# Spatial gate of a two-layer hybrid block: the bias as a tile added on VectorE, and the four mixing banks each behind another dense block

## The chip, the cores and the metric

The kernel runs on one NeuronCore of one Trainium2 chip. The metric is the device time of one launch in microseconds (us). The engines are TensorE (PE in the trace, its weight loads PEld), VectorE (DVE), ScalarE (ACT), GpSimd (POOL) and the DMA queues, issued by SyncE (SP). TensorE's granted clock is 1.00 (2.4 GHz) or 0.50 (1.2 GHz); a number between is a mean over a stretch.

## What is computed

Two layers on 1024 tokens of width 1024. The first projects the normalised input onto 7168 columns, runs four branches on parts of them (a short convolution, a stick-breaking attention, an RWKV-7 scan and a spatial gate), merges them under sigmoid gates, and ends with a gated feed-forward net with a convolution. The second is an attention layer. The change touches the spatial gate, branch four:

```python
def spatial_gating(z, ln_g, ln_b, w_s, b_s):
    u, v = jnp.split(jax.nn.gelu(z), 2, axis=-1)          # (1, 1024, 256) each
    v = layer_norm(v, ln_g, ln_b)
    vb = v.reshape(bsz, t // 128, 128, 4, 64)
    w_causal = jnp.tril(w_s)                               # (4, 128, 128)
    mixed = jnp.einsum('gts,bnsgc->bntgc', w_causal, vb) + b_s.T[:, :, None]
    return u * mixed.reshape(bsz, t, 256)
```

So in each of 8 groups of 128 positions, each of 4 channel groups of 64 is mixed over the positions by its own lower triangular 128x128 matrix; a bias that depends on the position in the group and the channel group is added; and the result is multiplied by u.

## The kernel before

**Dense blocks.** All large products are made of blocks. A block (`whole`, which calls `product`, lines 927 to 929) takes 1024x128 weights from a ring of two slots, each split into a high and a low part (`w_hi`, `w_lo`), and 8 x 2 x 3 = 48 products of 128x128 by 128x512: high by high, low by high, high by low, summed in PSUM. Its result [128 columns, 1024 tokens] lies in one of the two halves of the PSUM tile `gp` (block t in half t mod 2) and raises `p_ready`. ScalarE or VectorE takes it from there and raises `p_free0` or `p_free1`, for which block t+2 waits. GpSimd splits the weights of block t+1 once block t-1 is done; SyncE loads them from HBM (`w_raw`).

**The input projection** is 16 blocks (`for t in range(T_GATE)`), in the order of `IN_ORDER`: t = 0, 1 are u of the spatial gate (`y_d`), t = 2, 3 its v (`vt_sg`), t = 4, 5 the attention's v (`vt_sb`), t = 6 to 11 the short convolution (t = 10 and 11 are taken by VectorE, the others by ScalarE), t = 12 to 15 the attention's q and k. Then 32 gate blocks follow, of another loop, with pieces of the attention between their halves.

**Small work between the blocks.** The other half of PSUM is `sm`, four banks of [128, 512]. TensorE is given small work there between dense blocks, by hand: after t = 0 `col_turns` (parameters turned to columns), after t = 1 `bias_turns` (lines 1009 to 1015, the attention bias of the second layer, three products), after t = 4 and t = 7 `turn_v` (16 transposes each, v of the spatial gate and of the attention), and after t = 9 `sg_mix` (lines 1028 to 1043). Once VectorE has turned v to tokens x channels (line 2039), it normalises it in place in `v_sg` and raises `sg_normed` (line 2059).

`sg_mix` fills bank after bank, bank b = (ft, half) with channels 128 ft to 128 ft + 127 of tokens 512 half to 512 half + 511. A bank is four groups, one for each 128 tokens:

```python
pe.matmul(sm[:, b, c], group_sel[:, ft, :], sg_bias[:, :], start=True, stop=False, ...)       # line 1037
for hh in range(2):
    mm = pe.matmul(sm[C*hh:C*hh+C, b, c], v_sg[:, tt, C*g:C*g+C], w_sg[:, g, :], start=False, ...)  # line 1041
```

The first product puts the bias there: `group_sel` [4, 2, 128] selects for each channel its group's row of `sg_bias` [4, 128]. The other two are the mixing of two channel groups, which go to the two halves of the partitions. After a bank, `sg_mixed` goes up, and VectorE multiplies the bank by u into `y_d` (line 2071) and raises `sg_done`. Nothing before the first gate block waits for `sg_done`; there TensorE waits for four.

**VectorE's order** there is: `bias_vec` (line 2022) which SyncE stores and TensorE waits for ahead of `turn_v`; copies of v, its norm; v of the attention (line 2065, `v_taken`); the four gate products (line 2071); then for t = 10 and t = 11 the short convolution (lines 2078 to 2085), each of which first takes the block out of PSUM (line 2078) and so frees it.

Of the kernel before, what the change touches and what calls it, by code (L numbers as in the profile page):

```python
# [7 lines left out]
P = 128  # L8
# [6 lines left out]
BT = BW // P  # L15
C = 64
# [18 lines left out]
ALU = mybir.AluOpType  # L35
ACT = mybir.ActivationFunctionType
F32 = mybir.dt.float32
# [150 lines left out]
def hybrid_layers(nc, x, mix_norm_g, w_in, gate_b, sc_conv_w, sc_out, sb_out, rw_mu, rw_w0, rw_w2,  # L188
# [9 lines left out]
    with ExitStack() as ctx:  # L198
        base = [-(-nc.sbuf_base // 32) * 32]

        def at(name, shape, dtype, offset):
            return nc.alloc_sbuf_tensor_at(name, shape, dtype, offset=offset)
# [15 lines left out]
        group_sel = fixed("group_sel", [4, 2, P])  # L218
# [11 lines left out]
        sg_bias = fixed("sg_bias", [4, P])  # L230
# [42 lines left out]
        v_sg = at("v_sg", [P, NB, BW], F32, A0 + 40 * K)  # L273
        w_sg = at("w_sg", [P, 4, P], F32, A0 + 64 * K)
        gate_out = at("gate_out", [P, 2, T], F32, A0 + 56 * K)

# [636 lines left out]
        def _(pe):  # L913
# [94 lines left out]
            def bias_turns():  # L1008
                pe.wait_ge(s["rel_in"], 32)
                wait("wsg_copied")  # L1010
                wait("cols")
                for n in range(3):
                    mm = pe.matmul(sm[0:HEADS_A, n, 0:384], rel_rows[0:33, :],
                                   buckets[0:33, 384 * n:384 * n + 384], start=True, stop=True)
                mm.then_inc(s["bias_p"], 1)
# [11 lines left out]

            def sg_mix():
                wait("sg_normed")
                wait("wsg_ready")  # L1030
                pe.wait_ge(s["v_taken"], 8)
                for b in range(4):
                    ft, half = divmod(b, 2)
                    for n in range(4):
                        tt = 4 * half + n
                        c = slice(P * n, P * n + P)
                        pe.matmul(sm[:, b, c], group_sel[:, ft, :], sg_bias[:, :], start=True, stop=False,
                                  skip_group_check=True)
                        for hh in range(2):
                            g = 2 * ft + hh  # L1040
                            mm = pe.matmul(sm[C * hh:C * hh + C, b, c], v_sg[:, tt, C * g:C * g + C], w_sg[:, g, :],
                                           start=False, stop=True, skip_group_check=True)
                    mm.then_inc(s["sg_mixed"], 1)

            for t in range(T_GATE):
# [8 lines left out]
                if t == 7:  # L1054
                    pe.wait_ge(s["v_taken"], 4)
                    turn_v(vt_sb, 3)
                if t == 9:
                    sg_mix()

# [931 lines left out]
        def _(dve):  # L1991
# [19 lines left out]
            for i in range(16):  # L2011
# [8 lines left out]
            dve.tensor_copy(w_sg[:, :, :], sm[:, 1, :].rearrange("p (g t) -> p g t", g=4)).then_inc(s["wsg_copied"], 1)  # L2020
            wait("bias_p")
            dve.tensor_scalar(bias_vec[:, :].rearrange("p (n c) -> p n c", n=3), sm[0:HEADS_A, 0:3, 0:384],
                              -1.0, None, ALU.mult).then_inc(s["bias_rows"], 1)
# [38 lines left out]
            for b in range(4):  # L2062
# [3 lines left out]
                                sm[:, b, :].rearrange("p (n c) -> p n c", n=4)).then_inc(s["v_taken"], 1)  # L2066
            for b in range(4):
                ft, half = divmod(b, 2)
                c = slice(HALF * half, HALF * half + HALF)
                wait("sg_mixed")  # L2070
                dve.tensor_tensor(y_d[:, ft, c], sm[:, b, :], y_d[:, ft, c], ALU.mult).then_inc(s["sg_done"], 1)
            for n in range(2):
                t = IN_ORDER.index(4 + n)
# [7 lines left out]
                for shift in (1, 2):  # L2081
                    wait.after(dve.scalar_tensor_tensor(
                        acc[:, shift:T], cx[:, 0:T - shift], pcol("sc_w", 4 - 2 * shift + n),
                        acc[:, shift:T], ALU.mult, ALU.add))
                ins = dve.tensor_tensor(y_a[:, n, :], y_a[:, n, :], acc, ALU.mult)
            ins.then_inc(s["sc_done"], 1)

# [540 lines left out]
```

## Time and profile before

| | us |
|---|---|
| runs shown | 2606.4, 2625.24, 2626.96 |
| median of them | 2625.24 |
| the profiled execution, its own time | 2625.7 |
| span of its trace | 2623.8 |
| TensorE busy | 2508.9 (96%) |
| VectorE, ScalarE, GpSimd busy | 1051.2, 607.9, 823.9 |
| mean granted clock of TensorE | 0.971 |

The span is the time from the first to the last instruction in the trace; 1.9 us of the execution lie around it. Starts are counted from the span's start. Of TensorE's work the dense products of lines 927 to 929 are the most: 1600 of each line into `gp` and 352 into `sm`. A product of plain float32 operands stands in the trace as two instructions, so that one product of line 1037 reads "x2" and the two of line 1041 read "x4". The time that a product costs its successor is the distance of their starts; the duration in a row is longer, since products overlap.

### The profile page before, as it was taken

How to read it: one execution, taken by the hardware profiler on the slowest of the kernel's cores; microseconds unless marked ns; L12 is line 12 of the kernel's file. 1: busy time of each engine (PE TensorE's matmuls, PEld its weight loads, DVE VectorE, ACT ScalarE, POOL GpSimd, SP SyncE). 2: the span in 40 equal slices, each digit the busy share in tenths (PEclk: the TensorE clock that was granted, in tenths of full speed). 3: DMA queues.
4: the chain of work that ended last, by engine and by line, in shares of the span. 5: the costliest groups of instructions: out<-in, count | busy, mean ns of one | idle time of the engine just before them, and what ended most of it. 6: DMA issues, size and time to landing. Idle time of an engine off the chain costs nothing.

```text
span 2623.8 us, 36062 instructions
## 1 busy us (share of the span) xinstructions
PE 2508.9 (96%) x15586; PEld 1985.3 (76%) x15586; DVE 1051.2 (40%) x1275; ACT 607.9 (23%) x901; POOL 823.9 (31%) x518
## 2 busy tenths in 40 slices
PE   7999999999999979999999999999899989979998
PEld 6878777777778767888888888887677866646676
DVE  4211122241385264344444444444443216675521
ACT  3101122322222111121111111112322015554410
POOL 4312333233232057633333333332632310131221
PEclk9989999999999689999999999999999999989999
DMA  5111322222100055311111111111113122000023
GB/s 193 41 33 48 97 81 81 76 70 80 57 18 4 2 184 184 89 41 48 49 49 49 49 50 49 48 48 40 48 41 104 40 64 46 1 8 1 1 61 116
DMA packets 194122, 156.89 MB, mean 60 GB/s; under 512 B 15674, under 2 KB 175649, under 8 KB 193738
## 3 DMA queue, kind: packets, MB, share of 16 engines
q1 hardware_dynamic: 193994, 155.00, 19.5%
q8 instruction: 103, 1.69, 0.3%
q14 instruction: 25, 0.20, 0.0%
HBM read 125.58 MB, written 29.40 MB: 59 GB/s over the span
## 4 chain that ended last, share of the span: by engine, by line
PE 85%; DVE 8%; POOL 3%; ACT 2%; issue 1%; DMA 0%; SPq 0%; POOLq 0%; DVEq 0%; ACTq 0%
PE gp L927 18%; PE gp L929 17%; PE gp L928 17%; PE sm L929 4%; PE sm L927 4%; PE sm L928 4%; PE sm L1581 2%; PE gp L1484 2%; PE gp L1500 2%; POOL merged L824 2%; PE sm L1517 2%; DVE att_s L2466 1%; PE sm L1089 1%; PE sm L1439 1%; PE sm L1068 1%
## 5 line engine op out<-in xcount | busy, mean ns | idle before, releaser
L927 PE MATMUL gp<-h_hi,w_hi 128*128 128x512 f32 x1600 | 639.0, 399 | 1.3 <-ACT k_sb L1669 1.3
L929 PE MATMUL gp<-h_hi,w_lo 128*128 128x512 f32 x1600 | 624.3, 390 | 0.0
L928 PE MATMUL gp<-h_lo,w_hi 128*128 128x512 f32 x1600 | 624.0, 390 | 0.0
L726 POOL CAST w_hi<-w_raw 128x1024 fp32r<-128x1024 f32 (+1 forms) x165 | 176.1, 1067 | 1147.0 <-PE gp L929 821.0
L728 POOL TENSOR_TENSOR w_lo<-w_raw,w_hi 128x1024 fp32r<-128x1024 f32 x173 | 432.6, 2500 | 124.1 <-ACT w_hi L1822 101.9
L927 PEld LDWEIGHTS gp<-h_hi,w_hi 128*128 128x128 f32 x1600 | 301.0, 188 | 84.1 <-issue 23.6
L928 PEld LDWEIGHTS gp<-h_lo,w_hi 128*128 128x128 f32 x1600 | 301.1, 188 | 64.8 <-issue 4.5
L929 PEld LDWEIGHTS gp<-h_hi,w_lo 128*128 128x128 f32 x1600 | 300.9, 188 | 64.1
L2092 DVE TENSOR_TENSOR_SCAN sb_run<-sb_keep,ones_row 128x128 f32<-128x128 f32 (+7 forms) x32 | 77.1, 2449 | 318.2 <-POOL sb_keep L773 318.2
L927 PE MATMUL sm<-h_hi,w_hi 128*128 128x512 f32 x352 | 136.9, 389 | 0.0
L928 PE MATMUL sm<-h_lo,w_hi 128*128 128x512 f32 x352 | 136.9, 389 | 0.0
L929 PE MATMUL sm<-h_hi,w_lo 128*128 128x512 f32 x352 | 136.9, 389 | 0.0
L1929 ACT ACTIVATE att_s<-att_s,small 128x1024 f32<-128x1024 f32 (+7 forms) x128 | 98.7, 773 | 28.3 <-DVE small L2466 27.5
L1843 ACT ACTIVATE hid<-gp,col 128x1024 f32<-128x1024 f32 x22 | 24.6, 1119 | 325.9 <-DVE gp L2339 325.9
L1581 PE MATMUL sm<-k_tile,q_tile 96*128 96x512 f32 (+3 forms) x192 | 71.4, 509 | 20.0 <-DVE small L2466 13.9
L1484 PE MATMUL gp<-ident,att_s 128*128 128x128 f32 x576 | 79.0, 280 | 7.7 <-DVE att_pt L2486 7.7
L2339 DVE TENSOR_TENSOR gp<-gp,sin_t 128x1024 f32<-128x1024 f32 x22 | 27.1, 1233 | 131.0 <-PE gp L929 119.3
L1484 PEld LDWEIGHTS gp<-ident,att_s 128*128 128x128 f32 x576 | 61.7, 141 | 21.4 <-issue 10.3
L928 PEld LDWEIGHTS sm<-h_lo,w_hi 128*128 128x128 f32 x352 | 66.1, 188 | 13.7
L929 PEld LDWEIGHTS sm<-h_hi,w_lo 128*128 128x128 f32 x352 | 66.1, 188 | 13.7
L927 PEld LDWEIGHTS sm<-h_hi,w_hi 128*128 128x128 f32 x352 | 66.1, 188 | 13.7
L1941 ACT COPY att_pt<-gp 128x512 f32<-128x512 f32 (+1 forms) x80 | 45.0, 562 | 130.5 <-PE gp L1484 130.3
(475 smaller groups left out, 4111.6 us busy)
## 6 DMA issues: line engine op xcount, KB each, us to landing
w_raw<-in_w_in SPq DMA_DIRECT2D x79, 512.0 KB, 4.4
w_raw<-in_w_up SPq DMA_DIRECT2D x44, 512.0 KB, 3.8
gates_spill<-gate_out SPq DMA_DIRECT2D x32, 512.0 KB, 3.1
gate_in<-gates_spill SPq DMA_DIRECT2D x32, 512.0 KB, 4.3
w_raw<-in_w_down SPq DMA_DIRECT2D x22, 512.0 KB, 3.4
x_back<-x_spill SPq DMA_DIRECT2D x16, 512.0 KB, 4.2
x_tok<-in_x SPq DMA_DIRECT2D x8, 512.0 KB, 8.1
x_spill<-x_t SPq DMA_DIRECT2D x1, 4096.0 KB, 15.2
```

Of the source, the lines that this page charges most:

```text
L726: pool.tensor_copy(w_hi[:, t % 2, 0:n], w_raw[:, t % 2, 0:n]).then_inc(s["w_high"], 1)
L728: pool.tensor_tensor(w_lo[:, t % 2, 0:n], w_raw[:, t % 2, 0:n], w_hi[:, t % 2, 0:n].bitcast(F32), ALU.subtract).then_inc(s["w_split"], 1)
L824: pool.tensor_tensor(merged[:, d % 2, :], merged[:, d % 2, :], gated[:, q % 2, :], ALU.add) \
L927: pe.matmul(o, wh, hi[:, k0 + k, c], start=(k == 0), stop=False)
L928: pe.matmul(o, wh, lo[:, low[k] if low else k0 + k, c], start=False, stop=False)
L929: mm = pe.matmul(o, wl, hi[:, k0 + k, c], start=False, stop=(k == n - 1))
L1484: mm = pe.transpose(bank(4 + r % 3)[:, P * n:P * n + P], s_buf[:, u % 4, hh, P * k:P * k + P], ident[:, :])
L1500: mm = pe.matmul(at_o_place()[C * hh:C * hh + C, :], v[:, k, C * (2 * j + hh):C * (2 * j + hh) + C], pt_buf[:, u % 2, b, :], start=(k == 0 ...
L1517: return pe.matmul(o, q_2[rows, j, T - P * qb - P:T - P * qb], k_2[rows, j, a:a + m], start=True, stop=True)
L1581: return pe.matmul(o, q_tile[j][rows, hh, P * qb:P * qb + P], k_tile[rows, j, hh, a:a + m], start=True, stop=True)
L1929: act.activation(s_buf[:, u % 4, hh, 0:w], s_buf[:, u % 4, hh, 0:w], ACT.Exp, scale=-1.0, bias=at_small(0, u, hh), accum_out=at_small(1, u ...
L2092: ins = dve.tensor_tensor_scan(sb_run[:, hh, 0:w][:, ::-1], sb_keep[:, hh, 0:w][:, ::-1], ones_row[:, 0:w], 1.0, ALU.mult, ALU.mult)
```

## The change

Three things are altered. The bias is computed once, as a [128, 2, 128] tile: two products of `group_sel` and `sg_bias` go into bank 3 of `sm` at the head of `bias_turns`, and VectorE copies them to the new tile `sg_bias_t` ahead of `bias_vec`. The sixteen bias products in `sg_mix` are gone, and VectorE adds the tile to each bank in place, in PSUM, ahead of the product with u (`gate_mixed`). And `sg_mix(b)` issues one bank, behind blocks 8, 9, 10 and 11; on VectorE the banks 0 and 1 stand ahead of the convolution of t = 10, bank 2 behind it, and bank 3 behind that of t = 11.

```diff
+        sg_bias_t = at("sg_bias_t", [P, BT, P], F32, A0 + 66 * K + 512)
...
             def bias_turns():
                 wait("cols")
+                for ft in range(2):
+                    pe.matmul(sm[:, 3, P * ft:P * ft + P], group_sel[:, ft, :], sg_bias[:, :], start=True, stop=True)
...
-            def sg_mix():
-                wait("sg_normed")
-                wait("wsg_ready")
-                pe.wait_ge(s["v_taken"], 8)
-                for b in range(4):
-                    ft, half = divmod(b, 2)
-                    for n in range(4):
-                        tt = 4 * half + n
-                        c = slice(P * n, P * n + P)
-                        pe.matmul(sm[:, b, c], group_sel[:, ft, :], sg_bias[:, :], start=True, stop=False,
-                                  skip_group_check=True)
-                        for hh in range(2):
-                            g = 2 * ft + hh
-                            mm = pe.matmul(sm[C * hh:C * hh + C, b, c], v_sg[:, tt, C * g:C * g + C], w_sg[:, g, :],
-                                           start=False, stop=True, skip_group_check=True)
-                    mm.then_inc(s["sg_mixed"], 1)
+            def sg_mix(b):
+                if b == 0:
+                    wait("sg_normed")
+                    wait("wsg_ready")
+                    pe.wait_ge(s["v_taken"], 8)
+                ft, half = divmod(b, 2)
+                for n in range(4):
+                    tt = 4 * half + n
+                    c = slice(P * n, P * n + P)
+                    for hh in range(2):
+                        g = 2 * ft + hh
+                        mm = pe.matmul(sm[C * hh:C * hh + C, b, c], v_sg[:, tt, C * g:C * g + C], w_sg[:, g, :],
+                                       start=True, stop=True, skip_group_check=True)
+                mm.then_inc(s["sg_mixed"], 1)
...
-                if t == 9:
-                    sg_mix()
+                if 8 <= t < 12:
+                    sg_mix(t - 8)
...
             wait("bias_p")
+            wait.after(dve.tensor_copy(sg_bias_t[:, :, :], sm[:, 3, 0:2 * P].rearrange("p (f t) -> p f t", f=2)))
...
-            for b in range(4):
+            def gate_mixed(b):
                 ft, half = divmod(b, 2)
                 c = slice(HALF * half, HALF * half + HALF)
                 wait("sg_mixed")
+                mixed = sm[:, b, :].rearrange("p (n t) -> p n t", n=4)
+                wait.after(dve.tensor_tensor(mixed, mixed, sg_bias_t[:, ft, :].unsqueeze(1).to_broadcast([P, 4, P]),
+                                             ALU.add))
                 dve.tensor_tensor(y_d[:, ft, c], sm[:, b, :], y_d[:, ft, c], ALU.mult).then_inc(s["sg_done"], 1)
+            gate_mixed(0)
+            gate_mixed(1)
             for n in range(2):
...
                 ins = dve.tensor_tensor(y_a[:, n, :], y_a[:, n, :], acc, ALU.mult)
+                gate_mixed(2 + n)
             ins.then_inc(s["sc_done"], 1)
```

Where a row of the order of the changed kernel stands below, its line numbers are those of the changed kernel: its line 1042 is the mixing product (1041 before), 1014 the new bias product, 1016 the attention bias (1013 before).

On TensorE, the end of block 9 and the first groups of the mixing before; lines 928 to 929 are the dense products, 1037 a bias product, 1041 two mixing products:

```order
L927 MATMUL gp<-h_hi,w_hi 128x512
L928 MATMUL gp<-h_lo,w_hi 128x512
L929 MATMUL gp<-h_hi,w_lo 128x512
L1037 MATMUL sm<-sg_bias,group_sel 128x128
L1041 MATMUL sm<-w_sg,v_sg 64x128 x2
L1037 MATMUL sm<-sg_bias,group_sel 128x128
L1041 MATMUL sm<-w_sg,v_sg 64x128 x2
```

And the same engine at the end of block 8 now, where the first bank stands:

```order
L928 MATMUL gp<-h_hi,w_hi 128x512
L929 MATMUL gp<-h_lo,w_hi 128x512
L930 MATMUL gp<-h_hi,w_lo 128x512
L1042 MATMUL sm<-w_sg,v_sg 64x128 x8
L928 MATMUL gp<-h_hi,w_hi 128x512
L929 MATMUL gp<-h_lo,w_hi 128x512
L930 MATMUL gp<-h_hi,w_lo 128x512
```

The bias products are gone from between the mixing products, so eight of these stand together, and behind them the next dense block begins; the same eight stand behind blocks 9, 10 and 11.

On TensorE, at the end of block 1, before:

```order
L929 MATMUL gp<-h_hi,w_lo 128x512
L927 MATMUL gp<-h_hi,w_hi 128x512
L928 MATMUL gp<-h_lo,w_hi 128x512
L929 MATMUL gp<-h_hi,w_lo 128x512
L1013 MATMUL sm<-buckets,rel_rows 8x384 x3
L927 MATMUL gp<-h_hi,w_hi 128x512
```

And the same place now:

```order
L928 MATMUL gp<-h_hi,w_hi 128x512
L929 MATMUL gp<-h_lo,w_hi 128x512
L930 MATMUL gp<-h_hi,w_lo 128x512
L1014 MATMUL sm<-sg_bias,group_sel 128x128 x2
L1016 MATMUL sm<-buckets,rel_rows 8x384 x3
L928 MATMUL gp<-h_hi,w_hi 128x512
```

Two products of `sg_bias` have come ahead of the three of the attention bias.

On VectorE, from the attention's v (line 2065) to the second convolution block, with the semaphores that each waits for, before:

```order
L2065 COPY v_sb<-sm 128x4x128 [waits v_turned] x4
L2071 TENSOR_TENSOR y_d<-sm,y_d 128x512 [waits sg_mixed] x4
L2078 TENSOR_TENSOR sc_cx<-gp,sc_c 128x1024 [waits p_free1,p_free0,p_ready]
L2080 TENSOR_SCALAR sc_c<-sc_cx,col 128x1024 [waits p_free0]
L2082 SCALAR_TENSOR_TENSOR sc_c<-sc_cx,col,sc_c 128x1023 [waits dve_own]
L2082 SCALAR_TENSOR_TENSOR sc_c<-sc_cx,col,sc_c 128x1022 [waits dve_own]
L2085 TENSOR_TENSOR y_a<-y_a,sc_c 128x1024 [waits dve_own]
L2078 TENSOR_TENSOR sc_cx<-gp,sc_c 128x1024 [waits p_free1,p_free0,p_ready]
```

The same stretch now, from the first bank on:

```order
L2074 TENSOR_TENSOR sm<-sm,sg_bias_t 128x512 [waits sg_mixed]
L2076 TENSOR_TENSOR y_d<-sm,y_d 128x512 [waits dve_own]
L2074 TENSOR_TENSOR sm<-sm,sg_bias_t 128x512 [waits sg_mixed]
L2076 TENSOR_TENSOR y_d<-sm,y_d 128x512 [waits dve_own]
L2085 TENSOR_TENSOR sc_cx<-gp,sc_c 128x1024 [waits p_free1,p_free0,p_ready]
L2087 TENSOR_SCALAR sc_c<-sc_cx,col 128x1024 [waits p_free0]
L2089 SCALAR_TENSOR_TENSOR sc_c<-sc_cx,col,sc_c 128x1023 [waits dve_own]
L2089 SCALAR_TENSOR_TENSOR sc_c<-sc_cx,col,sc_c 128x1022 [waits dve_own]
L2092 TENSOR_TENSOR y_a<-y_a,sc_c 128x1024 [waits dve_own]
L2074 TENSOR_TENSOR sm<-sm,sg_bias_t 128x512 [waits sg_mixed]
L2076 TENSOR_TENSOR y_d<-sm,y_d 128x512 [waits dve_own]
L2085 TENSOR_TENSOR sc_cx<-gp,sc_c 128x1024 [waits p_free1,p_free0,p_ready]
```

Each bank has two operations where it had one, the add in place (line 2074) and the product with u (line 2076), and banks 2 and 3 stand behind the convolutions of t = 10 and t = 11.

## Rows read from the trace of the kernel before

**Rows 1.** The page's 40 slices of the span: granted TensorE clock, in tenths.
```profile
PEclk9989999999999689999999999999999999989999
```

**Rows 2.** Stretches of the input projection: from:to, length, busy and instructions by engine, clock, DMA.
```profile
60.00:151.00 91.00, 91.00 (x418) 75.40 (x416) 19.68 (x46) 8.63 (x9) 29.80 (x27) 1.00 0.17 47
151.00:155.00 4.00, 4.00 (x30) 2.45 (x30) 0.49 (x1) 1.01 (x1) 3.38 (x2) 0.99 0.00 0
155.00:175.40 20.40, 20.40 (x82) 12.90 (x81) 2.28 (x4) 0.00 (x0) 0.00 (x0) 0.50 0.09 27
```

**Rows 3.** Timeline of TensorE around the mixing: start, us, engine, line, operation, count.
```profile
150.95 0.39 PE L929 MATMUL gp<-h_hi,w_lo 128*128 128x512 f32 x1
...
151.26 0.48 PE L1037 MATMUL sm<-sg_bias,group_sel 4*128 4x128 f32 x2
...
151.68 0.44 PE L1041 MATMUL sm<-w_sg,v_sg 128*64 128x128 f32 x4
...
152.05 0.48 PE L1037 MATMUL sm<-sg_bias,group_sel 4*128 4x128 f32 x2
...
155.38 0.79 PE L1037 MATMUL sm<-sg_bias,group_sel 4*128 4x128 f32 x2
...
156.72 0.79 PE L1037 MATMUL sm<-sg_bias,group_sel 4*128 4x128 f32 x2
...
170.19 0.80 PE L927 MATMUL gp<-h_hi,w_hi 128*128 128x512 f32 x1
170.78 0.63 PE L928 MATMUL gp<-h_lo,w_hi 128*128 128x512 f32 x1
...
175.05 0.56 PE L929 MATMUL gp<-h_hi,w_lo 128*128 128x512 f32 x1
175.44 0.40 PE L927 MATMUL gp<-h_hi,w_hi 128*128 128x512 f32 x1
```

**Rows 4.** Timeline of TensorE around the transposes of `vt_sg`, and that stretch's clock.
```profile
93.24 1.91 PE L1024 MATMUL sm<-ident,vt_sg 128*128 128x128 f32 x16
94.90 0.48 PE L927 MATMUL gp<-h_hi,w_hi 128*128 128x512 f32 x1
95.22 0.40 PE L928 MATMUL gp<-h_lo,w_hi 128*128 128x512 f32 x1
...
93.30:97.30 4.00, 4.00 (x28) 3.60 (x27) 3.15 (x6) 1.02 (x1) 3.45 (x2) 1.00 0.01 2
```

**Rows 5.** Timeline of VectorE in the input projection.
```profile
60.57 1.35 DVE L2022 TENSOR_SCALAR bias_vec<-sm 8x1152 f32<-8x1152 f32 x1 [12.25 <-PE sm L1013]
...
128.29 2.48 DVE L2065 COPY v_sb<-sm 128x512 f32<-128x512 f32 x4 [0.65 <-PE sm L1024]
154.51 0.69 DVE L2071 TENSOR_TENSOR y_d<-sm,y_d 128x512 f32<-128x512 f32 x1 [23.74 <-PE sm L1041]
...
170.31 0.69 DVE L2071 TENSOR_TENSOR y_d<-sm,y_d 128x512 f32<-128x512 f32 x1 [4.70 <-PE sm L1041]
183.81 1.22 DVE L2078 TENSOR_TENSOR sc_cx<-gp,sc_c 128x1024 f32<-128x1024 f32 x1 [12.81 <-PE gp L929]
...
194.69 1.22 DVE L2078 TENSOR_TENSOR sc_cx<-gp,sc_c 128x1024 f32<-128x1024 f32 x1 [2.83 <-PE gp L929]
...
201.53 1.23 DVE L2085 TENSOR_TENSOR y_a<-y_a,sc_c 128x1024 f32<-128x1024 f32 x1
```

**Rows 6.** RWKV products and state loop: clock of two stretches and a gap, one step.
```profile
764.00:856.00 92.00, 85.72 (x2872) 81.89 (x2866) 49.03 (x59) 19.34 (x28) 27.09 (x14) 0.99 0.02 4
...
808.00:812.00 4.00, 2.56 (x142) 2.15 (x136) 4.00 (x5) 0.00 (x0) 0.15 (x1) 1.00 0.02 4
860.00:904.00 44.00, 41.71 (x728) 39.33 (x728) 5.33 (x30) 0.00 (x0) 0.00 (x0) 0.52 0.01 2
...
868.57 0.69 PE L1330 MATMUL sm<-s_all,s_step 64*64 64x64 f32 x8
...
871.57 0.69 PE L1330 MATMUL sm<-s_all,s_step 64*64 64x64 f32 x8
```

## The prediction

> **What bounds the kernel now.** I read the page first: TensorE is busy for 2508.9 of 2623.8 us, and the chain of waits that ended last is 85% TensorE's. So what counts is time taken out of TensorE's own stream, or a clock it gets back. The clock line [rows 1] shows mostly 9, with an 8 in the third slice (131 to 197 us), where the edited code stands. I then cut the input projection into stretches [rows 2]. From 60 to 151 us TensorE is busy for 91.00 of 91.00 us at clock 1.00. From 151 to 155, the first 4 us of the mixing, the clock is still 0.99. From 155 to 175.4 it is 0.50, with TensorE busy for all of the 20.40 us: it is not waiting for anything, it is slow.
>
> Next comes the timeline of that place [rows 3]. The mixing starts at 151.26, the next dense block at 170.19: 18.93 us for 16 groups. The first group takes 152.05 - 151.26 = 0.79 us, of which the bias product has 0.42 (to 151.68) and the two mixing products 0.37. Once the clock has fallen a group takes 156.72 - 155.38 = 1.34 us. The dense block that follows starts slow too: twelve products, from 170.19 to 175.05, at a pitch of (175.05 - 170.78) / 10 = 0.427 us. At full clock a block of 48 takes 194.69 - 183.81 = 10.88 us, two takings of blocks by VectorE [rows 5], or 0.227 each. The reader is to see that the stage costs 24.18 us up to 175.44, of which twelve dense products are worth 12 x 0.227 = 2.72, and that well over a third of the rest is the clock.
>
> VectorE waits for each bank: 23.74 us ahead of the first and 4.70 ahead of the last [rows 5]. It is off the path here.
>
> **What goes, TensorE.** All of 151.26 to 175.44 goes: 24.18 us.
>
> **What comes instead, TensorE.** Twelve dense products at full clock, 2.72 us. The mixing products, 16 groups x 0.37 = 5.92 us, if they keep the pitch they have beside a bias product and the clock stays up. For the clock the nearest row is the transposes of `vt_sg` [rows 4]: 94.90 - 93.24 = 1.66 us of small plain float32 work between dense blocks, and the clock over that stretch is 1.00. A bank alone is 4 x 0.37 = 1.48 us, shorter than that, with 10.88 us of dense work ahead of the next. The fall in rows 2 came some 4 us into the mixing. So I take full clock. Each of four pieces now has two edges. Entry: 151.26 - 150.95 = 0.31 against 0.227 [rows 3], 0.08 more. Exit: the first dense product after the transposes takes 95.22 - 94.90 = 0.32 [rows 4], 0.09 more. Four times 0.17 is 0.7. The two bias products in `bias_turns` cost 2 x 0.42 = 0.84, between dense blocks at full clock.
>
> Sum: 2.72 + 5.92 + 0.7 + 0.84 = 10.2 against 24.18, a gain of 14.0 us. The bounds: a group without its bias product can cost from 0.37 up to the whole 0.79 that it takes now, if the weight loads of the mixing had been hidden behind the bias product; that would be 16 x 0.42 = 6.7 us less gain. I take 0.37, since the weights of the second to fourth mixing instruction have no bias product ahead of them even now. On the other side the edges may cost nothing: 0.7 more. The gain lies between 7.3 and 14.7 if the clock stays up.
>
> **What comes on VectorE.** Four adds of 128x512 in place in PSUM. No such row is in the trace; nearest is the product with u, of the same size with one input in PSUM, 0.69 us [rows 5]. Below it could not go, as the size and the plain float32 operands are the same; above it, an output in PSUM could make it slower, say twice, 1.4. I take 0.7, so a bank costs 1.4 us where it cost 0.69. Order: banks 0 and 1 are done ahead of the taking of block 10 at 183.81; before it VectorE was idle for 12.81 us [rows 5]. Bank 2 stands behind the convolution of t = 10. That one runs from 183.81 for 8.05 us (VectorE's idle time ahead of the next taking is 2.83 us, out of 10.88). The block period is 10.88 + 1.48 + 0.17 = 12.5 us now, so the idle time of 2.83 grows to 4.5, and bank 2 needs 1.4 of it. The mixing of bank 2 ended before the convolution did. The queue behind it is the taking of block 11, for whose slot block 13 waits a whole block later. If the add took 3 us more than I think, it would still fit under that block. Bank 3 ends some 1.5 us after line 2085 of t = 11, at 201.53 + 1.23 before; TensorE first wants four `sg_done` at the gate blocks, four dense blocks or 43 us after block 11. All covered: cost 0.
>
> The bias copy is half the size of a copy at line 2065, four of which take 2.48 us [rows 5]: under 0.7 us, plus its wait. It delays `bias_vec` at 60.57 by at most 1 us, and with it SyncE's store, and the weight loads queued behind that store. TensorE wants `bias_rows` only at the transposes at 93.24 [rows 4], 31 us on. Cost 0. The first bank is mixed behind block 8, a block earlier: at 151.26 - 10.88 = 140.4 plus 0.84. The last thing that it waits for, the four copies of line 2065, ends at 128.29 + 2.48 = 130.77 [rows 5]: 10 us of room. Cost 0. Weight splits on GpSimd keep their place behind each block, and blocks now lie further apart; cost 0.
>
> **Sum against its own execution.** 2625.7 - 14.0 = 2611.7. The median shown, 2625.24, is 0.46 us below that execution; with that I forecast 2611.5, which is 0.5% faster. About 1% is what a measurement of this kernel tells from no change, so this reads as "same". With the bounds above it lies between 2610 and 2618.5.
>
> **Rivals.**
>
> State loop at full clock. From 860 to 904 us the RWKV state loop runs at clock 0.52 with TensorE busy for 41.71 of 44 us [rows 6], while the 92 us of small products of the same branch just ahead of it ran at 0.99. A step takes 871.57 - 868.57 = 3.0 us, and there are fourteen. At full clock TensorE's part halves; 41.71 / 2 is 21, and VectorE's part of each step does not shrink, so I estimate 20 us. For it: one of the three runs shown is 20.6 us shorter than the longest, the size of just this. Against it: the change does nothing to that stage but start it 14 us earlier. Time: 2611.5 - 20 = 2591.5.
>
> The fall is not the mixing's. If the clock falls around 155 us whatever TensorE is given, the 20.40 us at half clock now meet dense work and cost 10.2 of it. Gain 14.0 - 10.2 = 3.8, time 2621.4. For it: TensorE was busy throughout [rows 2], and so are dense blocks. Against it: 91 us of dense work at 1.00. A rule of the Trainium skill speaks on this rival's side ("TensorE: Matmul & The Clock Gate", section "Loop structure matters more than you think"): products that follow back to back keep the clock, and waits lose it. By that rule the mixing, back to back as it is, could not have lost it; the trace disagrees, 0.50 with no wait, and the measurement decides.
>
> Each piece takes the clock down. If 1.48 us of mixing is enough, a group's mixing products cost 1.34 x 0.37 / 0.79 = 0.63 us at half clock [rows 3], so each of the four pieces loses 4 x (0.63 - 0.37) = 1.0 us, and twelve dense products behind it 12 x (0.427 - 0.227) = 2.4. That is 3.4 x 4 = 13.6, and the time is 2625. Against it: rows 4.
>
> The slower one. A stage of small products can lose its clock earlier. From 764 to 856 us TensorE does the small products of the RWKV branch at 0.99; the clock falls only around 860. Between 808 and 812 us it is idle for 1.44 us of 4 and keeps 1.00 [rows 6]. If the new start of this stage, 14 us earlier, lets the clock fall in that gap, some 52 us, busy to 85.72 / 92 = 93%, run at half: 48 us more, 2611.5 + 48 = 2659.5. It decides against the change from a fall 15 us before 860 on. Against it: nothing in the edit touches that stage, and it kept its clock through that gap.
>
> **How the numbers follow.** Forecast 0.73; state loop at full clock 0.16; fall in any case 0.04; each piece falls 0.03; slower 0.04. The forecast's own range is 2608 to 2618.5. One run in three suggests that the first rival is real, so the range reaches to it, and up to the second: 2591 to 2622. Faster by over 1% (below 2599) is the state loop alone, 0.16; slower by over 1% 0.04; the rest, 0.80, within 1%.
>
> **What would show it.** TensorE's clock from 60 to 240 us at 1.00 throughout, with four pieces of about 1.5 us behind blocks 8 to 11, each ending in a dense product at a pitch of 0.3. The gate blocks begin 14 us earlier. Line 1041's products keep 0.37 per group. VectorE's adds take 0.7 us, and the taking of block 11 comes no later than its end. I am wrong if a piece takes over 2.5 us, if the clock falls between 140 and 190 us, or if the stage from 760 to 910 us differs from before by more than it should for a shift.

## The result, and the profile after

| | before | changed |
|---|---|---|
| runs | 20 | 20 |
| median, us | 2616.77 | 2599.83 |
| ratio of the two | | 0.9937, 95% interval 0.9915 to 0.996 |
| the profiled execution, us | 2625.7 | 2590.81 |
| mean granted clock in it | 0.971 | 0.983 |

The changed kernel is faster by 0.63%, with the interval clear of no change, though it is less than 1%. But the medians hide what happened, because both kernels have two run times. Of the 20 runs of before, ten lie at 2605 to 2611 us (median 2606.7) and nine at 2623 to 2628 (2625.2); one, at 4434, stands alone and is in neither group. Of the 20 of the changed kernel, ten lie at 2589 to 2592 (2590.8) and ten at 2607 to 2612 (2610.1). Short against short the change gives 15.9 us, long against long 15.1. Both profiled executions happen to differ in this too: before was a long one, the changed kernel a short one, so their difference of 34.9 us is not the change's. The mean granted clock of a run tells the two groups apart: in the runs of before that were timed beside the experiments it is 0.978 to 0.983 in short runs and 0.970 to 0.974 in long ones. So most of the rise from 0.971 to 0.983 in the table is not the change's either.

The page of the changed kernel: its span, and the clock in 40 slices, to be held against [rows 1]. The third slice is a 9 now.

```profile
span 2589.0 us, 36011 instructions
...
PEclk9999999999999999999999999999999989989999
```

Stretches of it: from:to, length, busy and instructions of TensorE, granted clock, DMA. They answer to [rows 2], and the last to the third line of [rows 6].

```profile
60.00:140.00 80.00, 80.00 (x369) 1.00 0.17 47
140.00:143.00 3.00, 3.00 (x26) 1.00 0.01 3
143.00:200.00 57.00, 57.00 (x284) 1.00 0.16 47
843.50:872.00 28.50, 24.92 (x729) 1.00 0.02 3
```

The clock is 1.00 through the whole input projection. It is 1.00 in the state loop too, where it was 0.52 in the execution of before. Cut finer, that execution shows that the loop, whose first product starts at 860.05, began at full clock and fell soon after (this view has the busy time of all engines ahead of the clock):

```profile
855.00:861.00 6.00, 4.48 (x213) 4.20 (x212) 3.46 (x5) 1.01 (x1) 0.00 (x0) 1.00 0.01 4
862.00:904.00 42.00, 39.77 (x673) 37.38 (x669) 4.97 (x28) 0.00 (x0) 0.00 (x0) 0.50 0.01 2
```

A step of that loop, in the timeline of TensorE, which answers to the last lines of [rows 6]:

```profile
845.89 0.45 PE L1331 MATMUL sm<-s_all,s_step 64*64 64x64 f32 x8
...
847.68 0.45 PE L1331 MATMUL sm<-s_all,s_step 64*64 64x64 f32 x8
```

847.68 - 845.89 = 1.79 us, against 3.0 at half clock. With 14 steps that is 17 us, and the two groups of runs lie 19 us apart. In all fourteen traces of this document the profiled run is a long one where the loop runs at half clock (before, and e1, e2, e8 and e12 below) and a short one where it runs at 1.00 (the other nine).

The first of the four mixing pieces, in the timeline of TensorE (line 1042 is the mixing product), which answers to [rows 3]:

```profile
140.16 0.39 PE L930 MATMUL gp<-h_hi,w_lo 128*128 128x512 f32 x1
140.48 1.09 PE L1042 MATMUL sm<-w_sg,v_sg 128*64 128x128 f32 x16
141.50 0.50 PE L928 MATMUL gp<-h_hi,w_hi 128*128 128x512 f32 x1
141.84 0.39 PE L929 MATMUL gp<-h_lo,w_hi 128*128 128x512 f32 x1
```

The piece takes 141.50 - 140.48 = 1.02 us for four groups, 0.255 each; I had put 0.37. Entry (0.32) and exit (0.34) are close to the 0.31 and 0.32 foreseen. The two bias products behind block 1, line 1014:

```profile
57.88 0.71 PE L1014 MATMUL sm<-sg_bias,group_sel 4*128 4x128 f32 x4
58.52 2.10 PE L1016 MATMUL sm<-buckets,rel_rows 33*8 33x384 f32 x6
```

58.52 - 57.88 = 0.64 us. And VectorE, which answers to [rows 5]: 2074 is the add, 2076 the product with u, 2085 the taking of blocks 10 and 11.

```profile
141.62 0.70 DVE L2074 TENSOR_TENSOR sm<-sm,sg_bias_t 128x512 f32<-128x512 f32 x1 [10.75 <-PE sm L1042]
142.35 0.69 DVE L2076 TENSOR_TENSOR y_d<-sm,y_d 128x512 f32<-128x512 f32 x1
...
164.84 1.23 DVE L2085 TENSOR_TENSOR sc_cx<-gp,sc_c 128x1024 f32<-128x1024 f32 x1 [9.67 <-PE gp L930]
...
172.83 0.69 DVE L2074 TENSOR_TENSOR sm<-sm,sg_bias_t 128x512 f32<-128x512 f32 x1
...
176.97 1.23 DVE L2085 TENSOR_TENSOR sc_cx<-gp,sc_c 128x1024 f32<-128x1024 f32 x1 [2.73 <-PE gp L930]
```

The add takes 0.69 to 0.70 us with its output in PSUM, like the product with u. The takings at 164.84 and 176.97 still wait for TensorE, for 9.67 and 2.73 us, and TensorE itself is busy without a gap from 60 to 200 us.

To compare kernels without the state loop I use one stage: from the first transpose of `vt_sg` (behind block 4) to the first attention score product (in the first gate block). It takes 162.77 us before (93.24, [rows 4], to 256.01) and 146.21 us in the changed kernel (93.33 to 239.54): 16.56 less. The two ends, before and changed:

```profile
256.01 0.49 PE L1068 MATMUL sm<-k_sb,q_sb 64*128 64x128 f32 x4
```

```profile
239.54 0.49 PE L1069 MATMUL sm<-k_sb,q_sb 64*128 64x128 f32 x4
```

The 0.64 us of the new bias products lie ahead of it, so the change is worth 16.56 - 0.64 = 15.9 us between these two traces, where the short runs say 15.9 and the long ones 15.1. The agreement to the tenth is partly luck: e11_before_fill, below, has the code of before in this stage, and its trace takes 161.32 us; the clock fell later there (156.8) and was low for 17 us, not 20. So a stage in which the clock falls can differ by over 1 us between executions. One in which it does not fall hardly does: the five kernels with all mixing behind block 9 and no bias products in it (e1, e7, e8, e10 and e12 below) took 145.08 to 145.14.

### The profile page after: what moved, and what is told of

It is laid out like the page before. It is cut to its first block, busy times and chain, and to the rows that moved or that the text cites. A ratio compares the mean times of both kernels' runs of the same rounds, so it can differ in the third digit from the quotient of the medians.

```text
span 2589.0 us, 36011 instructions
## 1 busy us (share of the span) xinstructions
PE 2474.2 (96%) x15558; PEld 1959.1 (76%) x15558; DVE 1053.5 (41%) x1280; ACT 608.2 (23%) x901; POOL 824.0 (32%) x518
## 4 chain that ended last, share of the span: by engine, by line
PE 85%; DVE 8%; POOL 3%; ACT 2%; issue 1%; DMA 0%; SPq 0%; POOLq 0%; DVEq 0%; ACTq 0%
PE gp L928 18%; PE gp L930 17%; PE gp L929 17%; PE sm L930 4%; PE sm L928 4%; PE sm L929 4%; PE sm L1582 2%; PE gp L1485 2%; PE gp L1501 2%; POOL merged L825 2%; PE sm L1518 2%; DVE att_s L2474 1%; PE sm L1090 1%; PE sm L1440 1%; PE sm L1069 1%
```

## The experiments

Twelve kernels ran. Their stage times, and all their runs, sorted into short and long ones by time and granted clock, with the medians in us. Five kernels were run once only. The edits below are shown in part ("..." marks what is left out) and against the changed kernel, unless before is named.

| kernel | stage, us | short runs | long runs |
|---|---|---|---|
| before | 162.77 | 10, 2606.7 | 9, 2625.2 |
| changed | 146.21 | 10, 2590.8 | 10, 2610.1 |
| e1_tile_only | 145.14 | 5, median 2587.9 | 3, 2607.2 |
| e2_split_only | 156.27 | 7, 2601.3 | 3, 2618.3 |
| e3_no_add | 146.25 | 1, 2589.2 | 0 |
| e4_two_places | 161.77 | 1, 2603.2 | 0 |
| e5_mix_twice | 148.63 | 1, 2596.0 | 0 |
| e6_full_rows | 153.90 | 1, 2598.8 | 0 |
| e9_zero_rows | 153.84 | 1, 2597.4 | 0 |
| e8_dma_tile | 145.14 | 7, 2589.3 | 5, 2607.9 |
| e7_fill | 145.09 | 7, 2591.2 | 0 |
| e10_dma_tile_fill | 145.14 | 8, 2589.8 | 0 |
| e11_before_fill | 161.32 | 12, 2608.4 | 0 |
| e12_thin_fill | 145.08 | 0 | 12, 2609.9 |

The runs of before and changed are those of the result. Before was timed again beside the experiments, in three sets. Medians of its short and long runs: beside e1 to e4, 2604.7 (5 runs) and 2624.3 (12); beside e5 to e8, 2607.1 (10) and 2625.9 (8); beside e9 to e12, 2606.4 (18) and 2626.1 (7).

### One part at a time

**e1_tile_only.** The bias tile, but all banks behind block 9, and VectorE's four gates ahead of the convolution.

```diff
-                if 8 <= t < 12:
-                    sg_mix(t - 8)
+                if t == 9:
+                    for b in range(4):
+                        sg_mix(b)
...
-            gate_mixed(0)
-            gate_mixed(1)
+            for b in range(4):
+                gate_mixed(b)
...
```

> The bias tile alone: no bias products in the mixing, but all four banks behind block 9 as before. Theory A (the clock falls because the stretch of small products lasts over some 4 us, and no bank alone does): 16 groups at 0.255 us are 4.1 us in a row, at the edge; the clock may fall near the end of the stretch or not at all, so the low clock costs between nothing and some 3 us of it. The time from the first transpose of vt_sg to the first attention score product is then 0.5 us shorter than in the changed kernel (three pieces fewer) up to 3 us longer. Rival B (the four-row bias products pull the clock down, not the length): clock 1.00 throughout, 0.5 us shorter. Rival C (the fall is tied to its place near 155 us and not to the mixing): clock 0.50 from some point near 155 us over 20 us of dense blocks, 10 us longer.

Measured: stage 145.14 us, 1.07 less than in the changed kernel. The timeline of TensorE there, and the clock of two stretches:

```profile
149.35 0.39 PE L930 MATMUL gp<-h_hi,w_lo 128*128 128x512 f32 x1
149.67 3.71 PE L1042 MATMUL sm<-w_sg,v_sg 128*64 128x128 f32 x64
153.31 0.50 PE L928 MATMUL gp<-h_hi,w_hi 128*128 128x512 f32 x1
```

```profile
149.00:155.00 6.00, 6.00 (x75) 1.00 0.05 15
155.00:161.00 6.00, 6.00 (x28) 1.00 0.26 75
```

All 16 groups take 153.31 - 149.67 = 3.64 us, 0.2275 each, and the clock stays at 1.00. So the tile alone brings 162.77 - 145.14 - 0.64 = 17.0 us, more than the whole change (the runs agree: 16.9 in the short ones, 17.1 in the long ones, against before beside it); on top of it the split costs 1.07 us: three more entries and exits at 0.2 over a dense product's pitch, and 4 x 1.02 - 3.64 = 0.44 inside the pieces. The place of the fall is not fixed in time either: rival C is out.

**e2_split_only.** One bank behind each of blocks 8 to 11, bias products and all; no tile, no add.

```diff
                 for n in range(4):
...
+                    pe.matmul(sm[:, b, c], group_sel[:, ft, :], sg_bias[:, :], start=True, stop=False,
+                              skip_group_check=True)
                     for hh in range(2):
...
-                                       start=True, stop=True, skip_group_check=True)
+                                       start=False, stop=True, skip_group_check=True)
...
-                wait.after(dve.tensor_tensor(mixed, mixed, sg_bias_t[:, ft, :].unsqueeze(1).to_broadcast([P, 4, P]),
-                                             ALU.add))
```

> The split alone: one bank behind each of blocks 8 to 11, with its bias products, no tile and no add on VectorE. A piece is some 3.1 us of small products (4 x 0.79). Theory A (length of the stretch): clock 1.00 throughout, every group 0.79 us, and the stage 16 x (0.79 - 0.255) - 0.64 = 7.9 us longer than in the changed kernel, so about half of the gain of 15.8 us comes from the split alone. Rival B (the four-row bias products pull the clock down): clock falls in or behind a piece at least once, the stage 10 us or more longer than in the changed kernel. Rival C (tied to the place): clock 0.50 for some 20 us near 155 us.

Measured: stage 156.27 us, so the split alone brings 6.5 us in this execution. A piece takes 3.1 us. Three keep the clock, but behind the second, which stood from 154.3 to 157.5, it fell for some 3 us. Clock of four stretches:

```profile
154.00:157.00 3.00, 3.00 (x22) 1.00 0.00 0
157.00:158.00 1.00, 1.00 (x8) 0.98 0.00 0
158.00:161.00 3.00, 3.00 (x8) 0.50 0.60 168
161.00:162.00 1.00, 1.00 (x5) 0.82 0.14 38
```

That speaks for rival B: 3.1 us with bias products lost the clock where 3.64 us without them did not. How often a piece loses it seems to vary from run to run: against before beside it, the long runs, of which this trace is one, gain 6.0 us, but the short ones only 3.4.

**e4_two_places.** As e2_split_only, but two banks behind block 8 and two behind block 10.

```diff
-                if 8 <= t < 12:
-                    sg_mix(t - 8)
+                if t in (8, 10):
+                    sg_mix(t - 8)
+                    sg_mix(t - 7)
```

> As the split alone, with bias products, but two banks behind block 8 and two behind block 10: two stretches of 6.3 us at full clock. Theory A (length): the clock falls in at least one of the two, some 4 us after its start, and comes back some 5 us into the next dense block; where it falls the stretch and the block behind cost 3 to 4 us more. Rival B, four-row products without regard to length: the same as in the split alone. If the clock stays 1.00 in both, 6.3 us is not long enough and theory A has its edge elsewhere.

Measured: stage 161.77 us, which lies within what the stage of before varies by (161.32 and 162.77), so nothing is shown to be gained. The clock falls in both stretches, which begin at 139.4 and 172.2:

```profile
139.00:142.00 3.00, 3.00 (x23) 1.00 0.01 3
144.00:152.00 8.00, 8.00 (x28) 0.50 0.23 66
172.00:176.00 4.00, 4.00 (x32) 1.00 0.00 0
178.00:182.00 4.00, 4.00 (x14) 0.50 0.24 73
```

**e3_no_add.** The changed kernel without VectorE's adds; the bias is left out.

```diff
-                wait.after(dve.tensor_tensor(mixed, mixed, sg_bias_t[:, ft, :].unsqueeze(1).to_broadcast([P, 4, P]),
-                                             ALU.add))
```

> The changed kernel without VectorE's four adds: the bias is left out of the result. Theory: the adds are off the path, so TensorE's stretch from the first transpose of vt_sg to the first attention score product is the same within 0.2 us. Rival (a piece or a block waits for VectorE): shorter by up to 2.8 us, four adds of 0.70.

Measured: stage 146.25 us against 146.21, so the adds cost nothing.

### What takes the clock down: length, or the four-row products

**e5_mix_twice.** e1_tile_only with every mixing product issued twice.

```diff
...
-                        mm = pe.matmul(sm[C * hh:C * hh + C, b, c], v_sg[:, tt, C * g:C * g + C], w_sg[:, g, :],
-                                       start=True, stop=True, skip_group_check=True)
+                        for again in range(2):
+                            mm = pe.matmul(sm[C * hh:C * hh + C, b, c], v_sg[:, tt, C * g:C * g + C], w_sg[:, g, :],
+                                           start=True, stop=True, skip_group_check=True)
...
```

> The bias tile alone, all four banks behind block 9, and every mixing product issued twice: a stretch of 7.3 us (32 x 0.2275) of mixing products without any bias product. Theory A (the length of a stretch of small products decides): the clock falls some 4 us into it and comes back some 5 us into the next dense block, so the stage is 3.64 us longer than the bias tile alone for the products and 5 to 7 more for the clock. Theory B (the bias products decide, four rows of the array and a gap of 0.17 us in the weight loads ahead of each): clock 1.00 throughout, the stage 3.64 us longer, 148.8 us.

Measured: stage 148.63 us, 3.49 more than e1_tile_only, about the 3.64 of the products added and nothing for the clock. One line of TensorE's timeline holds them all, and the clock stays:

```profile
152.53 7.26 PE L1043 MATMUL sm<-w_sg,v_sg 128*64 128x128 f32 x128
```

```profile
152.00:160.00 8.00, 8.00 (x132) 1.00 0.24 68
160.00:166.00 6.00, 6.00 (x28) 1.00 0.00 0
```

Over 7 us of small products in a row, and no fall. Theory A, the length of a stretch of small work, on which my prediction rested, is out.

**e6_full_rows.** The kernel before, with the bias products replaced by products of `ident` and `ones`: same count, same place, same size of output, but 128 rows of the array in place of four. The bias is 1 everywhere.

```diff
-                        pe.matmul(sm[:, b, c], group_sel[:, ft, :], sg_bias[:, :], start=True, stop=False,
+                        pe.matmul(sm[:, b, c], ident[:, :], ones[:, :], start=True, stop=False,
```

> The kernel before, with each bias product replaced by a product of the same size that uses all 128 rows of the array (ident by ones), so that the bias is 1 everywhere. Theory B1 (the four rows pull the clock down): clock 1.00 throughout, 16 groups at 0.79 or less, stage at least 8 us shorter than before, 154.6 us or less. Theory B2 (the gaps in the weight loads and the 0.37 us that a mixing pair takes beside a bias product do it, whatever the rows): clock 0.50 as before, stage within 1 us of 162.8.

Measured: stage 153.90 us, 8.87 less than before. Timeline of TensorE at the start and end of the mixing, and the clock over it and behind it:

```profile
151.21 0.38 PE L1037 MATMUL sm<-ones,ident 128*128 128x128 f32 x2
151.52 0.44 PE L1041 MATMUL sm<-w_sg,v_sg 128*64 128x128 f32 x4
151.89 0.49 PE L1037 MATMUL sm<-ones,ident 128*128 128x128 f32 x2
...
152.68 0.49 PE L1037 MATMUL sm<-ones,ident 128*128 128x128 f32 x2
...
162.91 0.49 PE L1037 MATMUL sm<-ones,ident 128*128 128x128 f32 x2
163.33 0.44 PE L1041 MATMUL sm<-w_sg,v_sg 128*64 128x128 f32 x4
```

```profile
151.00:164.00 13.00, 13.00 (x99) 1.00 0.15 42
164.00:180.00 16.00, 16.00 (x72) 1.00 0.01 2
```

The first full group takes 152.68 - 151.89 = 0.79 us, just as a group at full clock did in [rows 3]. But it goes on so for 12.5 us, and the clock never leaves 1.00. The number of products, their pitch, and the gap of 0.17 us in the weight loads ahead of each bias product, seen in both traces, are the same up to the fall; only the rows (and the data) differ.

**e9_zero_rows.** The same with a 128x128 tile of zeros in place of `ident`; the bias is left out.

```diff
...
-                        pe.matmul(sm[:, b, c], group_sel[:, ft, :], sg_bias[:, :], start=True, stop=False,
+                        pe.matmul(sm[:, b, c], zeros[:, :], ones[:, :], start=True, stop=False,
...
```

> The kernel before, with each bias product replaced by one of a 128x128 tile of zeros by ones: all 128 rows take part, but nothing is added, so the bias is left out. Theory B1a (what counts is how many rows the instruction names, not what is in them): clock 1.00 throughout, stage 153.9 us as with ident. Theory B1b (it is the switching of the data in the array): zeros are as quiet as four rows, the clock falls, stage 160 us or more.

Measured: stage 153.84 us, clock 1.00. The weights held nothing but zeros and the clock stayed, so it is not what the weights hold, but how many rows the product names. The other operand was ones in both e6_full_rows and e9_zero_rows; other contents of it, and numbers of rows between 4 and 128, were not tried here.

```profile
151.00:164.00 13.00, 13.00 (x98) 1.00 0.15 42
164.00:180.00 16.00, 16.00 (x72) 1.00 0.04 11
```

### The state loop

**e8_dma_tile.** e1_tile_only with the tile loaded by DMA, in place of two products and a copy.

```diff
...
-            sp.dma_start(sg_bias[:, :], sg_b[0]).then_inc(s["par_in"], 16)
+            for g in range(4):
+                sp.dma_start(sg_bias_t[C * (g % 2):C * (g % 2) + C, g // 2, :],
+                             sg_b[0][g].partition_broadcast(C)).then_inc(s["par_in"], 16)
...
```

> All four banks behind block 9 without bias products, and the tile loaded by four DMAs that spread a row of sg_b over 64 partitions each, in place of the DMA of sg_bias, the two bias products and VectorE's copy. Theory: 0.64 us off TensorE's stream against the bias tile alone, behind block 1, and nothing else; three more DMA issues of some 0.35 us each lie ahead of the load of the second weight block, which has room. Median of runs 0 to 2 us below the bias tile alone, and some 1.7 us below the changed kernel in runs of the same length of state loop. Rival: the second weight block comes late, and the start of block 1 moves by up to 1 us.

Measured: seven short runs at a median of 2589.3 us, five long ones at 2607.9; e1_tile_only had 2587.9 and 2607.2. The 0.64 us does not stand out in the runs, which spread over 4 us within one kind. The traces show it: from the first dense product to the first transpose it takes 92.20 - 34.43 = 57.77 us, against 93.33 - 34.92 = 58.41 in the changed kernel, so nothing was lost behind the DMAs.

What stands ahead of the loop in the kernels without a filling is a wait of 1.34 us for VectorE, in the changed kernel:

```profile
843.74 0.34 PE L1283 MATMUL sm<-v_tok,k_tok 64*64 64x64 f32 x4 [1.34 <-DVE zr L2253]
```

**e7_fill.** e1_tile_only with three products ahead of the state loop, into a bank that is written over later.

```diff
+            for n in range(3):
+                pe.matmul(sm[:, 0, :], ident[:, :], ones_row[:, 0:HALF], start=True, stop=True,
+                          skip_group_check=True)
             pe.wait_ge(s["rk_post1"], 6)
             rk_local(0)
```

> The bias tile alone, and three products of ident by ones (128x512) into bank 0 of sm, written over later, in the idle time of 1.34 us ahead of the RWKV state loop. Theory D (the clock in the state loop falls when TensorE has been idle just ahead of it): nearly all runs have the short loop, 2587 to 2593 us. Rival E (the loop's own products decide, or chance does): runs are split between some 2589 and 2607 us as in the other kernels, 18 us apart. The three products cost from 0 to 0.5 us.

**e12_thin_fill.** The same with `group_sel[:, 0, :]` and `ones_row[0:4, 0:HALF]`, so four rows.

> The bias tile alone, with three products in the same place that use four rows of the array (group_sel by ones, 128x512). They close the idle time as the full ones do. Theory D1 (idle time is what hurts): all runs in the short mode, near 2590 us. Theory D2 (few rows hurt as in the mixing, so thin products do not keep the clock): a split between 2590 and 2608 us as without them, or more runs in the long mode.

**e11_before_fill.** The kernel before with the three full products.

> The kernel before, with the three filling products alone. Theory D: all runs near 2606 us, none near 2625. Rival E: the split of the kernel before, about half and half.

**e10_dma_tile_fill.** e8_dma_tile with the three full products.

> The tile by DMA, all four banks behind block 9, and the three filling products ahead of the state loop. Theory D (the clock in the state loop falls after idle time just ahead of it): every run in the short mode, 2586 to 2592 us, against half of the runs without the filling. Rival E (chance): a split between some 2588 and 2608 us. Over the changed kernel's short runs a gain of 1 to 2 us, over its median some 10.

Measured: with the full products all runs are short, 7 of e7_fill, 8 of e10_dma_tile_fill and 12 of e11_before_fill. With the four-row ones all 12 of e12_thin_fill are long. Without a filling, before and the kernels made from it have 77 short runs and 57 long ones; before alone has 5 short of 17 in one set and 18 of 25 in another. Timeline of TensorE ahead of the loop, and the clock at its start and in it; first e7_fill (line 1323 is the filling, 1284 the loop's first product):

```profile
840.24 1.16 PE L1220 MATMUL gp<-rb_t,xa 64*64 64x64 f32 x64 [0.18 <-ACT xnv L1782]
841.33 2.84 PE L1323 MATMUL sm<-ones_row,ident 128*128 128x512 f32 x6
844.10 0.34 PE L1284 MATMUL sm<-v_tok,k_tok 64*64 64x64 f32 x4
```

```profile
842.00:846.00 4.00, 4.00 (x70) 1.00 0.00 0
846.00:872.00 26.00, 22.84 (x667) 1.00 0.01 4
```

Then e12_thin_fill:

```profile
841.32 2.84 PE L1323 MATMUL sm<-ones_row,group_sel 4*128 4x512 f32 x6
844.09 0.34 PE L1284 MATMUL sm<-v_tok,k_tok 64*64 64x64 f32 x4
```

```profile
842.00:846.00 4.00, 4.00 (x70) 1.00 0.00 0
846.00:850.00 4.00, 3.70 (x70) 0.54 0.02 4
850.00:880.00 30.00, 28.50 (x492) 0.50 0.01 2
```

The filling takes 844.10 - 841.33 = 2.77 us in the one and 844.09 - 841.32 = 2.77 in the other, at full clock in both. The loop begins at 1.00 in both; in e12_thin_fill it has fallen to 0.50 some 2 us after its first product, and from there to its end it stays. Theory D1 fell, and D2 holds. So theory D was half right: the moments ahead of the loop decide, but not by idle time alone, for closing it with thin products makes it worse. What decides between short and long in a kernel without a filling, all of whose runs are of the same program, stays open. The filling delays the loop: its first product comes 3.86 us after the start of line 1220's last group, against 843.74 - 841.24 = 2.50 in the changed kernel, 1.4 us that the short runs pay (e11_before_fill is at 2608.4, against 2606.4 in the short runs of before beside it, 2.0 more).

The version that is ahead of both kernels in the median is e10_dma_tile_fill: 2589.83 us over 8 runs (2586.5 to 2592.5), ratio to before 0.9912 (0.9881 to 0.9943), and some 10 us below the changed kernel's median, which was timed in another set. Nearly all of these 10 us come from having no long runs: the short runs of the changed kernel are at 2590.8, no further away than the spread, and so are those of e7_fill (2591.2).

## Why the prediction was right or wrong

**The stage (right in size, 1.9 us off).** I had 24.18 us going and 10.2 coming, a gain of 14.0; it is 15.9. The term that was mis-sized is the mixing products: 16 x 0.37 = 5.92 us, measured 4 x 1.02 = 4.08. The 0.37 was read beside a bias product; with none between them two mixing products take 0.2275 us in a row. I had bounded a group from 0.37 upward only, though nothing excluded less. The measured 15.9 lies outside the 7.3 to 14.7 within which I had put the gain. Next, 0.84 for the two bias products was 0.64. Edges, 0.7, were right: 4 x (0.32 + 0.34 - 2 x 0.227) = 0.8.

**"For the clock the nearest row is the transposes", so a short piece keeps it (right outcome, wrong reason).** The clock did stay at 1.00. But I gave the credit to the split, and it belongs to the bias products that went. The traces part the change so: the clock was 162.77 - 153.90 = 8.9 us (e6_full_rows; 7.4 if the 161.32 of e11_before_fill is taken for before), the bias products' own time 153.90 - 145.14 = 8.8, less 0.64 for making the tile, less 1.1 for the split. The split did nothing for the clock that the tile had not done (e1_tile_only, e5_mix_twice); alone, with the bias products, it kept the clock in three pieces of four in the one trace (e2_split_only), and its short runs gained only 3.4 us.

**The rule weighed there.** Against the rival in which the fall is not the mixing's, I set the Trainium skill, "TensorE: Matmul & The Clock Gate", section "Loop structure matters more than you think", beside 20.40 us at 0.50 without a wait, and the trace disagreed. It still does, for a stretch with products of four rows in it; back-to-back mixing products of 128 rows kept the clock over 7.2 us, as the rule has it.

**VectorE (right).** Adds of 0.7 us, all covered; taking them out changed the stage by 0.04 us. The taking of block 11 waited 2.73 us for TensorE, where I had 2.83 + 1.65 - 1.4 = 3.1.

**The state loop (the stage that moved the median).** I gave a chance of 0.16 to the rival in which it runs at full clock, and forecast 2611.5 from the long runs; these came at 2610.1. The rival's 2591.5 is where the short runs came, 2590.8. But it happens in half the runs, of both kernels. One of three runs shown was short, and I gave that less than one in three. So the median of 20 fell between the groups, 11.7 us below my forecast and outside the forecast's own 2608 to 2618.5; it lies in the full range only because I had let that reach to this rival. That a median of ten short and ten long runs falls between the groups is chance, and no merit of the forecast. One sign of being wrong came true by this: the stage from 760 to 910 us differs between the two profiled executions by more than a shift. It is no effect of the change: short and long runs are 10 to 9 and 10 to 10.

**The other rivals.** The fall tied to its place, and each piece taking the clock down, did not happen. The slower one, an earlier fall among the RWKV products that costs 48 us, was seen in no run of the changed kernel: none lies above the long group. A brief fall there does occur: in the trace of e8_dma_tile the clock was 0.59 from 794 to 798 us and 1.00 again from 798 to 800.

## What to carry to other kernels

If the granted clock falls while TensorE is never idle, look at how many rows its products name: sixteen bias products of four rows cost 7.4 to 8.9 us in clock, about as much as in their own time (8.8). Put such an add on an engine with time to spare. Giving the product 128 rows kept the clock too, with zeros for weights as well; the bias itself, filled up with zeros to 128 rows, was not run. And before splitting a stretch of small work, try it whole without its worst part: here the split cost 1.1 us that nothing gave back.

Where one kernel has two run times, find the place where the two part before comparing medians; here what TensorE did in the last 2.8 us ahead of a long loop of small products decided over 19 us, and full-row products put there settled it, at 1.4 us of delay.

## What the runs showed of the hardware that was not expected

- Same count, pitch and gaps: with four-row products between the mixing products the clock fell to 0.50 some 3.5 to 6 us after the first of them (before, e2_split_only, e4_two_places, e11_before_fill); with 128-row products it stayed at 1.00 over 12.5 us (e6_full_rows), and so it did with weights of zeros (e9_zero_rows).
- The loop of 64x64 products began at 1.00, and either kept it to its end, for 25 us, or fell within some 2 us and ran the rest, 42 us, at 0.50. What stood ahead of it for 2.77 us decided: 27 of 27 runs short behind 128-row products, 12 of 12 long behind four-row ones, 77 short and 57 long behind 1.34 us of idle time.
- A pair of plain float32 mixing products (64 columns of weights) costs 0.2275 us among its like and 0.37 next to a product with 128 columns of weights, whether this has four rows or 128 ([rows 3] and e6_full_rows). Why was not tried.
- An add of 128x512 with one input and the output in PSUM takes 0.69 to 0.70 us on VectorE, as the product from PSUM to SBUF does (0.69).
